# The experts' keys stay in the tenth row of a gather ring, and nine rows are left for gathers

## What is computed

```python
def one_block(xb):
    q = (xb @ q_w).reshape(PEER_BLOCK, PEER_HEADS, 2, PEER_DQ // 2)
    s = jnp.einsum('thcd,hcnd->thcn', q, sub_keys).astype(jnp.float32)
    s1, i1 = lax.top_k(s[:, :, 0], PEER_TOPK)
    s2, i2 = lax.top_k(s[:, :, 1], PEER_TOPK)
    ...
    top_s, pos = lax.top_k(cand, PEER_TOPK)
    eidx = jnp.take_along_axis(cidx, pos, axis=-1)
    g = jax.nn.softmax(top_s, axis=-1)
    u = eu[eidx]
    v = ev[eidx]
    a = jax.nn.gelu(jnp.einsum('td,thkd->thk', xb, u).astype(jnp.float32))
    return jnp.einsum('thk,thkd->td', (g * a).astype(v.dtype), v)
```

## Time and profile before

| | us |
|---|---|
| median of 3 runs (lowest to highest) | 1937.91 (1937.32 to 1948.46) |
| the profiled execution | 1946.51 |
| its span, first to last instruction | 1944.6 |
| PE matmul busy | 1490.2 (77%) |
| DVE busy | 1258.6 (65%) |
| POOL busy | 783.3 (40%) |
| ACT busy | 763.5 (39%) |

### The profile page before, as it was taken

One profiled execution on the slowest core, in us unless ns is written; L12 is line 12 of the kernel. 1 busy time (PEld: TensorE's weight loads), 2 busy tenths in 40 slices (PEclk: granted clock), 3 DMA queues, 4 the chain that ended last, 5 costly groups with the idle time before them and its releaser, 6 DMA issues.

```text
span 1944.6 us, 27857 instructions
## 1 busy us (share of the span) xinstructions
PE 1490.2 (77%) x9567; PEld 832.6 (43%) x9567; DVE 1258.6 (65%) x3411; ACT 763.5 (39%) x2179; POOL 783.3 (40%) x676
## 2 busy tenths in 40 slices
PE   7868777969689988869668879689789785866535
PEld 4747643436345533446214447345455242423101
DVE  1565777945878788845986655984565645443755
ACT  1431345742355567642246642232222323232322
POOL 0000234423234354522443334776565767422532
PEclk9989887888789998978868989889899777786858
DMA  9986999989999999999999999999999999999997
GB/s 395 335 318 233 420 408 419 421 337 415 415 387 405 410 420 403 375 421 420 419 421 398 420 420 419 390 390 401 360 379 387 360 398 348 402 410 392 382 414 301
DMA packets 133447, 756.73 MB, mean 389 GB/s; under 512 B 17182, under 2 KB 36542, under 8 KB 47282
## 3 DMA queue, kind: packets, MB, share of 16 engines
q0 software_dynamic: 82432, 578.86, 73.7%
q1 hardware_dynamic: 50875, 176.10, 23.4%
HBM read 750.19 MB, written 9.29 MB: 391 GB/s over the span
## 4 chain that ended last, share of the span: by engine, by line
PE 29%; DVE 19%; DMA 18%; issue 7%; ACT 6%; POOL 5%; another core or an unknown queue 1%; SPq 0%; ACTq 0%; DVEq 0%
PE bank L1463 11%; DMA expert_rows<-in_expert_uv,expert_index 10%; DVE expert_rows L2768 8%; PE bank L1206 3%; POOL weight_units L2816 3%; PE bank L860 3%; PE bank L1334 3%; POOL expert_rows L2812 2%; PE bank L1190 2%; PE bank L797 2%; DMA weight_units<-in_w_out_units 2%; DMA weight_units<-in_peer_q_units 1%; DMA gate_or_shift_and_scale<-mod_dram 1%; DVE gate_or_shift_and_scale L2226 1%
## 5 line engine op out<-in xcount | busy, mean ns | idle before, releaser
L2812 POOL DMA_INDIRECT expert_rows<-in_expert_uv,expert_index x544 | 641.4, 1179 | 1095.2 <-PE bank L1463 747.7
L2768 DVE CUSTOM_DVE_ANT_0 expert_rows<-expert_rows,h_rows 128x1024 f32<-128x1024 f32 x544 | 660.6, 1222 | 300.3 <-DMA expert_rows<-in_expert_uv,expert_index 280.9
L1463 PE MATMUL bank<-expert_rows,weight_diagonals 64*64 64x512 f32 x4096 | 605.0, 708 | 143.0 <-ACT weight_diagonals L2048 130.0
L2028 ACT ACTIVATE group_gelu<-group_dots 128x2 f32<-128x2 f32 x272 | 55.8, 205 | 757.8 <-DVE group_dots L2768 677.2
L1463 PEld LDWEIGHTS bank<-expert_rows,weight_diagonals 64*64 64x64 f32 x4096 | 153.9, 151 | 430.5 <-issue 237.9
L2048 ACT ACTIVATE weight_diagonals<-consts_sb,group_weights 128x64 f32<-128x64 f32 (+1 forms) x544 | 159.0, 340 | 16.7 <-ACT group_weights L2038 0.7
L1206 PE MATMUL bank<-stage_room,weight_units 128*128 128x128 f32 x1024 | 129.2, 286 | 13.9 <-ACT stage_room L1867 7.4
L1206 PEld LDWEIGHTS bank<-stage_room,weight_units 128*128 128x128 f32 x1024 | 122.7, 199 | 34.9 <-issue 22.1
L2038 ACT ACTIVATE group_weights<-group_gelu,expert_gate 128x1 f32<-128x1 f32 x544 | 131.6, 289 | 9.4
L2028 ACT ACT_TABLE_LOAD x74 | 94.9, 1283 | 1.3
L2226 DVE SCALAR_TENSOR_TENSOR conv_out<-stage_room,small_weights,conv_out 128x128 f32<-128x128 f32 (+1 forms) x360 | 94.9, 310 | 0.1
(11 more groups left out here) (392 smaller groups left out, 1983.1 us busy)
## 6 DMA issues: line engine op xcount, KB each, us to landing
weight_units<-in_peer_q_units SPq DMA_DIRECT2D x40, 1024.0 KB
weight_units<-in_w_in_units SPq DMA_DIRECT2D x23, 1024.0 KB
weight_units<-in_w_out_units SPq DMA_DIRECT2D x19, 1024.0 KB
weight_units<-in_w_ada_units SPq DMA_DIRECT2D x13, 1024.0 KB
expert_rows<-in_expert_uv,expert_index POOLq DMA_INDIRECT x544
weight_units<-in_w_units SPq DMA_DIRECT2D x8, 1024.0 KB
expert_rows<-in_w_ada_units SPq DMA_DIRECT2D x7, 1024.0 KB, 11.0
gate_or_shift_and_scale<-mod_dram SPq DMA_DIRECT2D x11, 512.0 KB
```

The source lines that it names most:

```text
L1463: last = mm(e.bank[2 * a + c][o * HD:(o + 1) * HD, :], e.diag[ps, m % (NG * GR)], e.ring[ps, m % RING, cs], start=first, stop=final)
L2028: do(e.act_v[:, p], e.dots[:, p], ACT.Gelu_apprx_tanh).then_inc(e.s_gelu, 1)
L2768: vec.tensor_tensor_reduce(out=row, in0=row, in1=e.h2[:, i % 2], scale=1.0, scalar=0.0, op0=ALU.mult, op1=ALU.add, accum_out=e.dots[:, q % ...
L2812: pool.indirect_dma_start(e.ring[:, n % RING], None, e.io["expert_uv"], bass.IndirectOffsetOnAxis(ap=e.eidx[:, i % 2, j:j + 1], axis=0)).t ...
```

## The change

The two halves of the keys are loaded once, at the same two places in SP's program as before, into the ring's tenth row, and stay there for all five tiles. RING becomes 9, so the gathers use nine rows. The eight key units go from the list of units, and with them their waits on PE and on SP; the units behind them move up, so that many sit in another slot. PE waits for one semaphore per half, which stays raised.

```diff
-RING = 10
+RING = 9
...
-    e.ring = e.sb("expert_rows", [P, RING, 2 * D])
+    e.ring = e.sb("expert_rows", [P, RING + 1, 2 * D])
+    e.keys = [e.ring[:, RING, half * D:(half + 1) * D] for half in range(2)]
...
-        "query0": lambda i: [("pq", i, u) for u in range(4)] + ([("keys", i, 0)] if 0 < i < PT else []),
-        "query1": lambda i: ([("pq", i, u) for u in range(4, 8)] + ([("keys", i, 0)] if i == PT else [])
-                             + ([("keys", i, 1)] if i else [])),
+        "query0": lambda i: [("pq", i, u) for u in range(4)],
+        "query1": lambda i: [("pq", i, u) for u in range(4, 8)],
...
-    def key_half(i, half):
-        if i == 0:
-            pe.wait_ge(e.s_k0[half], 16)
-            return (e.mod_a, e.mod_b)[half].rearrange("p (a n) -> p a n", a=PH)
-        return units.take(("keys", i, half))[:, 0:D].rearrange("p (a n) -> p a n", a=PH)
+    def key_half(half):
+        pe.wait_ge(e.s_k0[half], 16)
+        return e.keys[half].rearrange("p (a n) -> p a n", a=PH)
...
-            if q and i:
-                units.used_by(("scores", i, 2 * half + 1))
...
         if key == ("pq", 0, 2):
             sp.wait_ge(e.s_x1, 1)
-            sp.dma_start(e.mod_a, io["keys_unit"][:, 0:D]).then_inc(e.s_k0[0], 16)
+            sp.dma_start(e.keys[0], io["keys_unit"][:, 0:D]).then_inc(e.s_k0[0], 16)
         if key == ("pq", 0, 3):
             sp.wait_ge(e.s_h2, 1)
-            sp.dma_start(e.mod_b, io["keys_unit"][:, D:]).then_inc(e.s_k0[1], 16)
+            sp.dma_start(e.keys[1], io["keys_unit"][:, D:]).then_inc(e.s_k0[1], 16)
```

More of the change, by code:

```diff
@@ L1251, in sample_queries @@
         yield
-    def key_half(i, half):
-        if i == 0:
-            pe.wait_ge(e.s_k0[half], 16)
-            return (e.mod_a, e.mod_b)[half].rearrange("p (a n) -> p a n", a=PH)
-        return units.take(("keys", i, half))[:, 0:D].rearrange("p (a n) -> p a n", a=PH)
+    def key_half(half):
+        pe.wait_ge(e.s_k0[half], 16)
+        return e.keys[half].rearrange("p (a n) -> p a n", a=PH)
     def scores_of(i, half):
-        keys = key_half(i, half)
+        keys = key_half(half)
         prod.freed(pe, ("pq", i, 2 * half + 1))
@@ L1288, in query0 @@
                 if q == 0:
-                    keys = key_half(i, 0)
+                    keys = key_half(0)
                 prod.freed(pe, ("pq", i, q))
@@ L1315, in query1 @@
                                   e.q2T_s[:, 8 * half + 4 * q + a, 0:NS], keys[:, 4 * q + a], start=True, stop=True)
[L1316 to L1320, removed]
+            last.then_inc(prod.ready, 1)
     def sc(part):
@@ L2843, in load_unit @@
             sp.dma_start(slot, io["peer_q_units"][key[2]]).then_inc(sem, 16)
-        elif kind == "keys":
-            sp.dma_start(slot[:, 0:D], io["keys_unit"][:, key[2] * D:(key[2] + 1) * D]).then_inc(sem, 16)
         elif kind == "pages":
@@ L3098, in build @@
         e.s_tap = e.sem("conv_taps_added")
-        e.s_k0 = [e.sem(f"first_keys_loaded{half}") for half in range(2)]
+        e.s_k0 = [e.sem(f"keys_loaded{half}") for half in range(2)]
         e.s_sx0 = e.sem("first_two_heads_shifted")
```

## The result

| | before | changed |
|---|---|---|
| median, first comparison (4 runs each) | 1937.62 us | 1964.36 us (1961.05 to 1966.38) |
| ratio, first comparison | | 1.0095, 95% interval [1.006, 1.013] |
| median, again on another chip (31 and 8 runs) | 1942.37 us | 1958.29 us |
| ratio, again | | 1.0084 [1.0055, 1.0113] |
| the profiled execution | 1946.51 us | 1964.4 us |

The changed kernel is slower, by a little under 1%. By the ratios that is +16.3 us (0.0084 x 1942.37) to +18.4 us (0.0095 x 1937.62). The two medians of the first comparison, of four runs each, lie further apart than its ratio, 26.7 us (1.0138), and why is not shown; in the second, with more runs, medians (1.0082) and ratio agree, so I go by the ratios. The forecast was +5.1 us and a median of 1943.0, with a range of 1922 to 1962. The first median lies 2.4 us above the range.

The account below looks back on a forecast made before the run. Bound: the nearly full DMA in query stages, PE in other stretches, DMA shared with POOL's page requests in the sample's. Terms +7.5 - 7.5 + 0 + 2.5 + 2.6 = +5.1 us on 1937.9 gave 1943.0 us, range 1922 to 1962.

Parts of the forecast that it names:

- The key waits: PE's six waits before the scores, 17.4 us, read as waits for key halves: they vanish, priced 0, bounds 0 and -17.4.
- the second argument: Behind PE's waits before the scores, a gather issued earlier into a full queue would stand longer, not land earlier: 0.
- The bytes of the keys: Tiles 1 to 3, saturated query stages: two key halves fewer each, 3 x 1.049 MB less on the DMA, -7.5 us.
- The query stages of tiles 1 to 3: Saturated DMA stages: with nine rows one row fewer is in store before each, 3 x 2.5 = +7.5 us.
- The PE-bound stretch: Such as 577.6 to 804 us: rows lie ready and DVE does not wait, so one row less costs 0.
- POOL's queue in the sample's stretch: Page requests stand behind gathers that wait for a freed row; PE's one long page wait grows, +2.6 us.
- Its bound of +10: Upper bound for the sample's stretch: all four streaks of POOL's page requests pay 2.6 us, about +10 us.
- The end: From about 1824 us to the last gather, DMA saturated: one row more must come in, +2.5 us.
- The sign that I gave for it: Time from POOL's last long wait (1824.43) to the end, 120.2 us before, would grow by about 2.5.
- Lookahead decides: Slower rival: at 1400 to 1650 us the ring of rows sets the pace, 250 us times 10/9, 1968.2 us; chance 0.14.
- Its sign: DVE's waits for gathered rows rising by more than 30 us would show that lookahead decided.
- The rule on repeated gaps: Repeated gaps on the engine to be saturated can mean too few buffers; nine rows should open more; kept as slow rival.

Follow-up runs that it names:

- ring10_keys_stay: Against the kernel before: ten gather rows, keys of tiles 1 to 4 kept where heads 0 to 3's bias stood, no key units; 0.998, -3.9 us.
- ahead8_100_to_179: The kernel before, but for gathers 100 to 179 POOL waits for two more freed rows, as with eight; 1.0, 0 us.
- ahead9_from_384: The kernel before, but from gather 384 on POOL waits for one more freed row, as with nine; 1.0039, +7.6 us.
- ring9_key_units: The kernel before with nine gather rows, keys still loaded again for each tile as units; 1.0112, +21.8 us.
- after_again: The changed kernel unchanged, run again on another chip as a control, against the kernel before; 1.0084.
- after_fewer_stores: The changed kernel without four stores of tiles 2 and 3 to new_win_prompt, against the kernel before; 1.011.

## Why the prediction was right in sign and too small

**The key waits: a wrong reading, and a right price by luck of the second argument.** Six waits at L1265 have no releaser, and I took the nearest load for it. I said that they would vanish, and they did not: 22.5 us in the changed kernel, and 20.4 in the one with ten rows and resident keys. One of the six in the changed kernel, where the keys have lain in memory for 700 us, shows the real chain. DVE, ACT and PE, three timelines:

```profile
911.04 1.22 DVE L2760 CUSTOM_DVE_ANT_0 expert_rows<-expert_rows,h_rows 128x1024 f32<-128x1024 f32 x1 [3.62 <-DMA expert_rows<-in_expert_uv,expert_index]
```

```profile
912.31 0.20 ACT L2020 ACTIVATE group_gelu<-group_dots 128x2 f32<-128x2 f32 x1 [7.93 <-DVE group_dots L2760]
912.55 0.48 ACT L2030 ACTIVATE group_weights<-group_gelu,expert_gate 128x1 f32<-128x1 f32 x2
912.93 0.56 ACT L1915 COPY stage_room<-bank 128x512 f32<-128x512 f32 x1
```

```profile
913.60 2.05 PE L1263 MATMUL bank<-expert_rows,stage_room 128*128 128x128 f32 x8 [5.58 <-issue]
```

PE has its queries ready at 908.0. The copy of them (L1915) stands in ACT's program behind a gelu, the gelu waits for DVE's dots, and DVE for a gathered row. The side work of a query stage hangs on the rows too. The kernel before shows the same ahead of the wait that ends at 903.41:

```profile
902.12 0.21 ACT L2028 ACTIVATE group_gelu<-group_dots 128x2 f32<-128x2 f32 x1 [6.07 <-DVE group_dots L2768]
902.75 0.56 ACT L1923 COPY stage_room<-bank 128x512 f32<-128x512 f32 x1
```

I took 0 for these waits because a gather in a full queue comes behind them, and 0 was measured when they shrank by 7 us.

**The bytes of the keys (-7.5 us).** Too large by the middle values: -3.9 by ring10_keys_stay, and 1.0095 and 1.0084 beside 1.0112 say much the same, -3.3 and -5.4. The interval (-9.6 to +1.6) holds -7.5 as well. 4.19 MB less is 10 us of DMA. In the one profile of ring10_keys_stay the DMA is busy 14 us less than before and idle 17 us more, so the bytes that are gone leave idle time behind. That the keys were worth their bytes only where the DMA was the bound just then is my reading.

**The query stages of tiles 1 to 3 (+7.5 us).** +10.6 us (5.3 to 15.8) was measured for all rows to 383, so the size is about right. Where it is lost the profiles show only in part. Of all on record, six have nine rows' lookahead up to row 383 and six ten throughout it. The mean step of the six with nine less that of the six with ten is +3.1, +0.9 and +0.2 us in the rows beside the three stages (55 to 103, 191 to 231, 287 to 323), but also +3.6 from 223 to 287, where I had no term, and -4.4 from 323 to 383. Only the first is clear of the spread: 175.7 to 179.5 us with nine, 172.0 to 176.5 with ten. So a loss in the query stage of tile 1 is shown; that each of the three stages costs 2.5 us is not, and where the rest of the 10.6 us is lost stays open.

**The PE-bound stretch (0).** Right, and shown with two rows less (-4.5 to +4.7 us). That DVE never waits for rows there was wrong (10.8 us in the changed kernel), but 23.2 us of such waits cost ahead8_100_to_179 nothing.

**POOL's queue in the sample's stretch (+2.6 us).** By the profiles this step failed most. I followed one page back through POOL's program, and took one of four streaks, because PE shows one long wait. The stretch lost 8.7 us in the profiles (row 399 to 463, 204.63 us as the mean of six with ten, 213.35 of five with nine) and some 5.6 by the clock (7.6 of ahead9_from_384, less 2.0 of the end; the interval of the 7.6 is 1.4 to 13.9). Its bound of +10 was the better value. The loss shows as more waits and not as a longer one. In the changed kernel they are for SP's loads behind the pages too, and over all profiles more than half of them are for DVE and ACT, a path that the step didn't have.

**The end (+2.5 us).** Right. From the use of row 495 to the end seven profiles with ten rows' lookahead take 119.4 to 121.2 us (mean 120.1), six with nine 121.3 to 122.5 (mean 122.1), that with eight 129.7. The DMA is full there (0.99 and 1.00), which fits that the row that isn't in store has to come. The sign that I gave for it, the time from POOL's last long wait, grew by only 0.8 us in the one pair of profiles.

**Lookahead decides (rival, 0.14, 1968.2).** By the numbers the truth lies between it and the forecast. Its place was half right: 1400 to 1650 us lost the most by the profiles, but 10.6 of 18.2 us by the clock were lost up to row 383, before about 1450 us. Its price, 1/10 of the time, was not: 205 us became 214, not 228. Its sign, DVE's waits up by over 30 us, fired; but ahead8_100_to_179 has 350.8 us of them and loses nothing, and only 23 of these fall in the rows whose lookahead was cut. That sign was badly chosen.

**The rule on repeated gaps** (the Trainium skill, Perfetto Trace Analysis, Optimization Strategy), which says they can mean too few buffers, I kept only as the slow rival, because the DMA share showed none. At a share of 0.98 over 1944.6 us, 49 us were idle, and 77 us with nine rows. Over all profiles the DMA is idle 42 to 60 us in the five kernels with key units and ten rows (one of them with eight for rows 100 to 179), 62 to 77 in the five with nine throughout, and 110 with eight. But ring10_keys_stay has 66 us and loses nothing, so idle time goes with the loss and is not yet its price. The rule was right about the direction, and the eight-row kernel bears it out.

**Added up:** the forecast's ring terms make +12.6 and were measured as +18.2 in two parts and as +21.8 at once, with an interval (13.7 to 30.2) that leaves +12.6 out; its keys -7.5, measured -3.9. That gives +14 to +18 for both, and +16 to +18 was seen. So what is shown is that the ring's price was too small; of its two parts (rows to 383, and from 384 on) and of the keys each forecast lies inside its interval.

**What stays open.** From row 335 to 383 (1287 to 1440 us) the kernel before takes 153 us and the changed one 146. All profiles with ten rows' lookahead there (seven) take 140 to 163 us, those with nine (six) 144 to 149, so it is not the ring. The kernel before has a PE wait of 13.47 us there behind DVE; what releases DVE was not found. How the loss divides among late rows, late pages and DVE's and ACT's side work in rows 399 to 463 was not found either. Nor was a longer ring tried, for want of memory.

## What to carry to other kernels

Here a ring between a nearly full DMA and its consumers could not be cut for free, though a DMA share of 0.98 looks full. The tenth row was worth 18 to 22 us here and the ninth about 50, so the price of the next one cannot be read off the last. Look at the DMA's idle time in all stretches together, and count every streak of requests that stands behind it in a queue. When a wait has no releaser, follow the in-order program of the engine that feeds it before naming a load; and take the longest new wait of a profile away before calling it the cause.

## What the hardware showed that I had not expected

**Small stores go one for one with large gathers.** The stores that DVE waits for are descriptors of 512 B, 0.03 us each in the records, beside 8 KB gather descriptors of 0.31 us. Counted over 3 us from 739 us on:

```
changed:  138 of 512 B stores,  146 of 8 KB gathers
before:   351 of 512 B stores,  122 of 8 KB gathers
```

In the changed kernel the two go one for one, and the stores move 0.07 MB in 3 us. In the kernel before they do so too from 730 to 733 us (144 and 143). At the end of the changed kernel's stores, from 753.4 to 757.2 us, the stores' records come in groups of a few at once, 0.30 to 0.35 us apart, which is about the length of one gather descriptor. A store of 2 KB (four descriptors), issued behind its like, took 23.65 us in this way. Why the stores of the kernel before rush through from 739 us on, three to one, is not shown. By 735.51 us POOL has waited 9.70 and 4.88 us for PE there, and its next two gathers take 3.46 and 2.59 us to issue; that the gathers' queue ran low is my reading, and it was not tried. In the changed kernel POOL has waited nearly as long, 8.65 and 4.18 us. The Trainium skill (DMA: Bandwidth & Descriptors, Queues, rings and completion order) has each DMA engine take turns between the queues it has work for, packet by packet, and calls some 9 to 17 descriptors typical for a packet. The count agrees with turns, and it gives both queues equally many descriptors a turn; the spacing at the end fits a packet of one descriptor here.

**A wait of ten microseconds comes and goes.** From row 159 to row 175 the kernel before takes 46.2 us, the changed one 57.0, ring9_key_units 45.4, ring10_keys_stay 55.4, after_again 58.9 and after_fewer_stores 45.8. The medians do not follow it. One profile of each kernel doesn't place a loss of this size; groups of them do, as in rows 399 to 463, where six with ten rows' lookahead take 202.1 to 207.1 us (mean 204.6) and five with nine 208.4 to 216.0 (mean 213.4), the pages in their old place in all.
